# Late conditioning products at steps 3 to 28, 59 and 64 of the second block's input product, weights rounded one piece a step, and GpSimd's loads in that order

## What is computed

```python
mod = c_act @ w_ada[l] + b_ada[l]          # 1024 x 6144 weights
sh1, sc1, g1, sh2, sc2, g2 = jnp.split(mod, 6, axis=-1)
h = rmsnorm(x, norm1_g[l]) * (1.0 + sc1[:, None, :]) + sh1[:, None, :]
proj = h @ w_in[l]                         # 1024 x 5120 weights
q_m, k_m, v_m, q_d, k_d, v_d, gate_m, gate_d = jnp.split(proj, IN_SPLITS, axis=-1)
# rotary embedding on q_m, k_m, q_d, k_d; causal attention of both kinds;
# merged = sigmoid(gate_m) * y_m + sigmoid(gate_d) * y_d; x = x + g1 * (merged @ w_out)
# then a mixture of 32 experts, each with three matrices of 2 MB, and a last norm
```

## Time and profile before

| | |
|---|---|
| median of 3 runs | 1083.11 us (1081.07 to 1083.81) |
| profiled execution | 1078.99 us, span 1077.2 us |
| mean granted clock of TensorE | 0.946 |
| TensorE busy | 914.2 us (85%) |
| VectorE busy | 540.8 us (50%) |
| ScalarE busy | 347.3 us (32%) |
| DMA | 316.71 MB, mean 294 GB/s |

### The profile page before, as it was taken

How to read it: one execution, slowest core, us unless ns; L and a number is a source line. 1 busy time by engine, 2 the same in 40 slices (tenths; PEclk the granted TensorE clock), 3 DMA queues, 4 the chain that set the end, 5 groups by cost and what they waited for, 6 DMA issues and landing times.

```text
span 1077.2 us, 19224 instructions
## 1 busy us (share of the span) xinstructions
PE 914.2 (85%) x8378; PEld 703.1 (65%) x8378; DVE 540.8 (50%) x1008; ACT 347.3 (32%) x684; POOL 76.3 (7%) x113
## 2 busy tenths in 40 slices
PE   8999999999999999999999998766666666657665
PEld 7587888489999888988989965433334333334332
DVE  2465588858888766888757643211112111212121
ACT  3420255247776536455553341000001000000001
POOL 3111710000000000330010000000000000000000
PEclk9999999999999999999999999988889788988888
DMA  9434472685554564875536999999999999999994
GB/s 343 148 138 145 148 257 83 231 277 173 176 164 176 201 236 182 271 241 193 176 130 243 429 389 415 428 427 431 428 429 426 430 430 429 428 430 427 427 431 195
DMA packets 76106, 316.71 MB, mean 294 GB/s; under 512 B 3999, under 2 KB 27840, under 8 KB 63472
## 3 DMA queue, kind: packets, MB, share of 16 engines
q1 hardware_dynamic: 71252, 302.24, 71.4%
q0 software_dynamic: 4624, 13.14, 4.0%
q10 hardware_dynamic: 140, 0.04, 0.0%
HBM read 312.24 MB, written 1.06 MB: 291 GB/s over the span
## 4 chain that ended last, share of the span: by engine, by line
PE 56%; DMA 29%; DVE 8%; ACT 4%; issue 2%; SPq 1%; POOL 0%; DVEq 0%; ACTq 0%
PE ps L463 54%; DMA w<-in_w_up 20%; DMA w<-in_w_gate 6%; DMA w<-in_w_down 2%; DVE sp L1861 1%; DMA w<-in_w_in 1%; DMA rot<-q 1%; PE ps L589 0%; PE ps L2703 0%; DVE acc L925 0%; ACT sp L1852 0%; ACT sd L2184 0%; PE ps L2116 0%; SPq L3003 0%; SPq L3028 0%
## 5 line engine op out<-in xcount | busy, mean ns | idle before, releaser
L463 PE MATMUL ps<-w,xg 128*32 128x256 f32 x2048 | 158.1, 472 | 106.4 <-DMA w<-in_w_up 83.1
L463 PE MATMUL ps<-hb,sp 128*128 128x256 f32 x1824 | 224.6, 283 | 0.0
L463 PEld LDWEIGHTS ps<-hb,sp 128*128 128x128 f32 x1824 | 218.7, 188 | 3.9 <-issue 2.8
L463 PEld LDWEIGHTS ps<-w,xg 128*32 128x32 f32 x2048 | 84.4, 131 | 178.9 <-issue 154.7
L1861 DVE TENSOR_TENSOR sp<-w,sp 128x1024 fp32r<-128x1024 f32 x122 | 144.4, 1219 | 37.1 <-ACT sp L1852 37.1
L1852 ACT ACTIVATE sp<-w 128x1024 fp32r<-128x1024 f32 x122 | 122.1, 1051 | 41.5 <-PE ps L463 40.5
L2877 DVE TENSOR_TENSOR cst<-ps,cst 64x256 f32<-64x256 f32 x31 | 13.3, 428 | 222.2 <-ACT cst L2797 222.2
L2797 ACT ACTIVATE cst<-ps 64x256 f32<-64x256 f32 x31 | 11.7, 378 | 324.0 <-PE ps L463 324.0
L2903 DVE TENSOR_TENSOR ost<-ps,cst 32x256 f32<-32x256 f32 x120 | 50.4, 420 | 101.0 <-PE ps L463 98.2
L463 PE MATMUL ps<-w,hts 128*32 128x256 f32 x1024 | 63.0, 386 | 13.4 <-ACT hts L2810 11.4
L463 PE MATMUL ps<-ht,w 128*128 128x256 f32 x256 | 60.4, 386 | 2.8 <-ACT sq L709 1.7
(11 more groups left out here) (415 smaller groups left out, 1163.1 us busy)
## 6 DMA issues: line engine op xcount, KB each, us to landing
w<-in_w_down SPq DMA_DIRECT2D x36, 2048.0 KB, 35.2
w<-in_w_gate SPq DMA_DIRECT2D x32, 2048.0 KB, 28.2
w<-in_w_up SPq DMA_DIRECT2D x32, 2048.0 KB, 32.6
w<-in_w_in SPq DMA_DIRECT2D x13, 2048.0 KB, 9.9
w<-in_w_up SPq DMA_DIRECT2D x22, 1024.0 KB, 7.7
w<-in_w_ada SPq DMA_DIRECT2D x8, 2048.0 KB, 8.0
w<-in_w_out SPq DMA_DIRECT2D x4, 2048.0 KB, 9.1
w<-in_w_ada POOLq DMA_DIRECT2D x8, 768.0 KB, 5.0
```

Of the source, the lines that this page charges most:

```text
L463: return q.eng.matmul(o, l, r, start=start, stop=stop, skip_group_check=True)
```

## The change

Parts 4 to 11 of the late conditioning products are run by VectorE at steps 3, 8, 13, 18, 23, 28, 59 and 64 in place of 3, 11, 19, 27, 35, 43, 51 and 59. ScalarE rounds the second piece of a half one step after the first. GpSimd's order becomes: loads 0 to 6, rotation 2, load 7, rotation 3, load 8, rotation 4, load 9, rotation 5, load 10, rotations 6 to 9, load 11.

```diff
+        LATE_AT = (3, 8, 13, 18, 23, 28, 59, 64)
...
         def proj2_sc(q):
...
-                if g % 4 == 0 and 0 < g <= 80:
-                    split_sc(q, 35 + g // 4)
+                if g % 4 < 2 and 0 < g // 4 <= 20:
+                    split_sc(q, 35 + g // 4, (g % 4,))
...
         def proj2_ve(q, late_ada):
...
-                if g % 8 == 3:
+                if g in LATE_AT:
                     next(late_ada, END)
                 if g % 4 in (1, 2) and 0 < g // 4 <= 20:
                     split_ve(q, 35 + g // 4, (g % 4 - 1,))
...
         # GpSimd
-            for n in range(6):
+            for n in range(7):
                 ada_late_gp(q, n)
-            rotate_gp(q, 2)
-            for n in range(6, 9):
-                ada_late_gp(q, n)
-                rotate_gp(q, 2 * n - 9)
-                rotate_gp(q, 2 * n - 8)
-            ada_late_gp(q, 9)
-            rotate_gp(q, 9)
-            for n in (10, 11):
-                ada_late_gp(q, n)
+            for r in range(2, 6):
+                rotate_gp(q, r)
+                ada_late_gp(q, r + 5)
+            for r in range(6, 10):
+                rotate_gp(q, r)
+            ada_late_gp(q, 11)
             router_gp(q)
```

## The result

The changed kernel takes 1095.31 us (median of 5 runs, 1093.96 to 1096.87), the kernel before 1083.11 in the 5 runs beside them (1080.59 to 1085.32). The ratio is 1.0124, with a 95% interval of 1.0109 to 1.0139: slower; the medians are 12.2 us apart, and the interval is 11.8 to 15.1 us. The forecast was 1088.0, +4.9, in a range that ended at 1094.0. The direction was right; the size was less than half of what came, and the time lies 1.3 us above the range.

What follows compares the result with a forecast made beforehand. TensorE was taken as full to 465.52, with VectorE's rotary half 5 due then without slack. Delay 6.3, plus clock 0.7, less 1.05 and 1.0, gives +4.9 us: 1088.0 from 1083.11, range 1081.0 to 1094.0.

Steps and rivals of the forecast that it cites:

- the landing of loads 6 to 9: GpSimd's late loads, issue to landing: 6.0 us for 768 KB and 4.3 for 512 KB in the middle estimate.
- the loop: Load n waits for product n-1, VectorE for the load: 7.2 to 9.4 us a 768 KB link against 7.1 of room.
- my middle case: Late loads land in 6.0 us (512 KB: 4.3), load 6 at 444.1; rotary half 5 is 6.4 us late at step 31.
- My high case: Late loads land in 7.0 us (512 KB: 4.8), half 5 is 9.3 late; with 2.3 for rotation 6, +11.3 in all.
- These 2 MB loads start up to 8 us later and still land before their pieces are due: The step's own input-weight loads, delayed by late pieces, would be in time even at 12.7 us of landing.
- Rotation 6 behind load 10: Rotation 6, now issued behind load 10, might land late too: 2.3 us, counted only in the high sum.
- The 1.05 behind product 9: TensorE's other idle time between 465.52 and 503.90, behind product 9 on VectorE, should go: -1.05 us.
- the 1.0 from ScalarE's pd: TensorE's 1.28 us wait for ScalarE's pd at 544.60 should fall by one rounded piece: -1.0 us.
- The 1.34: TensorE's 1.34 us wait at 477.71 for VectorE's normalisation, expected to fall away against the clock's cost.
- The clock: After some 6 us of stall at step 31 TensorE's lower clock costs 2.0 us, net 0.7 less the wait at 477.71.
- The shift one for one: A TensorE delay at the end of the 84 steps reaches the kernel's end whole, as the experts' stream shifts with it.
- The 3.8 us for 768 KB: Skill's rule for late loads, 2.0 us plus bytes at 436 GB/s: half 5 only 1.2 us late, kernel 1080.6.

Runs made afterwards that it cites:

- e1_split_only: Kernel before with only ScalarE's second rounded piece one step later: 1080.8 us against 1082.88, ratio 0.9991.
- e3_rot_first: Changed kernel with each GpSimd rotation issued ahead of the load it stood behind: 1094.79 us against 1081.07 for the kernel before, ratio 1.0127.
- e7_late_end: Kernel before with the rounding edit, products 8 to 11 at steps 59, 64, 69, 74, loads 9 to 11 behind all rotations: 1080.53 us, ratio 0.9987.
- e6_two_places: Changed kernel with loads 5, 7 and 9 in a second place, so load n waits for product n - 2: 1083.07 us, ratio 1.0006 to the kernel before.
- e10_all_small: Changed kernel, loads 5 to 10 and input weights of halves 39 to 46 cut to 64 of 512 columns: scores +0.3 us, end of steps -2.4.
- e2_late_only: Changed kernel with ScalarE rounding both pieces in one step again: 1096.38 us against 1082.88 for the kernel before, ratio 1.0117.
- e4_small_loads: Changed kernel with loads 5 to 10 cut to 64 of 512 columns: 1088.03 us against 1082.88 for the kernel before, ratio 1.0045.
- e9_filler17: Changed kernel with 17 unused fp32 matmuls in TensorE's wait before the first scores: 1095.7 us against 1080.81 for the kernel before, ratio 1.0133.
- e11_cut4: Changed kernel with the 2 MB input-weight loads of halves 39 to 46 issued as four 512 KB loads: 1094.73 us, ratio 1.0111 to the kernel before.
- e12_cut8: Changed kernel with the 2 MB input-weight loads of halves 39 to 46 issued as eight 256 KB loads: 1096.37 us, ratio 1.0144 to the kernel before.

## Why the forecast was right in kind and wrong in size

**The step that failed** is the landing of loads 6 to 9, taken at 6.0 us (4.3 for load 8). They took 8.8, 6.1, 6.6 and 6.6. With these four put into the prediction's own links, from the issue of load 6 at 438.68 on, half 5 ends at 477.6; it ended at 477.7. So the loop and its other terms were right, and this one was mis-sized.

| | forecast (middle) | measured |
|---|---|---|
| waits at steps 8, 13, 18, 23, 28 | 2, 4, 1, 0, 1 | 2.06, 6.92, 1.11, 1.61, 2.75 |
| loads 6 to 9 issued | 438.1, 446.5, 455, 461.8 | 438.68, 449.85, 458.62, 467.11 |
| half 5 late at step 31 | 6.3 | 11.9 |

Load 6 brings 2.8 of the 5.6 us that were missing at step 31, loads 8 and 9 the most of the rest: load 8 had been taken as in time, and 1.61 us were waited for it. (The loss at the end of the steps, 12.9, is 8.0 above the forecast; the other 2.4 lie behind the scores, where 1.35 should have come back and 1.0 was lost. They are told below.) I had the row for load 6 in the earlier trace rows (7.0 us, beside a 2 MB load), took a middle between it and the quickest, and read it as a price per load. It is a landing behind another transfer: the load issued 1.8 us earlier lands 1.2 us earlier at the median and no earlier in the execution profiled here, so that its price grows by a part or all of what it is moved forward. From the kernel before, 447.0 could have been read as the time near which load 6 lands, 2.9 us later than the 444.1 of my middle case; the six traces with the new order have 446.2 to 447.0. And 7.0 us was the least of four: with rotation 2 ahead of it load 6 took 7.6, 8.2 and 7.5 in e1_split_only, e3_rot_first and e7_late_end. My high case (7.0 for each load of 768 KB, 4.8 for load 8) reached 9.3 and was too low as well.

**"These 2 MB loads start up to 8 us later and still land before their pieces are due"** was wrong. VectorE's late pieces delay the load that takes their slot, from 441.12 to 451.85; behind load 7 it takes 11.7 us and lands at 463.5, where ScalarE has waited for it. ScalarE's timeline:

```profile
445.68 2.01 ACT L1852 ACTIVATE sp<-w 128x1024 fp32r<-128x1024 f32 x2 [1.82 <-DMA w<-in_w_in]
...
463.54 2.01 ACT L1852 ACTIVATE sp<-w 128x1024 fp32r<-128x1024 f32 x2 [6.20 <-DMA w<-in_w_in]
```

TensorE didn't run out of pieces there, as it stood before its scores. But load 8 (458.62) and load 9 (467.11) again met one of these loads in flight: from 458 to 460 us SyncE's queue has 371 records and GpSimd's 1. The loop keeps itself going: a late product delays a piece, the piece a 2 MB load, and that one the next late load.

**The loop itself** (load n behind product n - 1, VectorE in order, the rotary work behind it) was right, and the direction of the result with it: e6_two_places, which cuts it, takes away 10.7 of the 11.9 us; e10_all_small, which makes its links short, 11.6.

**Rotation 6 behind load 10**, the 2.3 us that only the high case held, came: VectorE waits 2.62 us for it and TensorE 2.18 at 492.45. e3_rot_first, which turns the order round, takes both away.

**What is given back.** TensorE's idle time behind the first scores was 3.67 and is 3.04 (2.18, 0.17, 0.35, 0.34). The 1.05 behind product 9 went but for 0.17; the 1.0 from ScalarE's pd came, less what a second such wait took, and was shown alone in e1_split_only. The 1.34 was to go and is replaced by the 2.18.

**The clock.** It fell to 0.50 within the wait of 8.06 us (the window 474 to 476 shows 0.67, 476 to 478 shows 0.50). From there 4 and 36 matmuls took 0.80 and 5.85 us; before, the same 4 took 0.49 and the 36 behind them 4.53. That is 1.6 us where I took 2.0, and with 0.6 less idle time it makes the 1.0 by which the loss grows from the scores (11.9) to the end of the steps (12.9). Whether it cost time here is open: at 492.45 TensorE waits for VectorE anyway. In e3_rot_first, without that wait, such a fall cost 1.85.

**The shift one for one.** The first expert load is issued at 578.37 before and 591.71 after, 13.3 us later, and over the runs the stage and the kernel go together: +12.9 and +12.2, e2_late_only +13.8 and +13.5, e4_small_loads +5.1 and +5.2, e6_two_places -0.5 and +0.2. The experts' stream absorbs nothing, as forecast.

**The 3.8 us for 768 KB** of the Trainium skill (DMA: Bandwidth & Descriptors, Anatomy of one DMA), by which half 5 would have been 1.2 us late: the quickest load of that size here took 4.8 us before, and 5.5 with the 2 MB loads cut. For 96 KB the same rule gives an estimate of 2.2 us, and the traces, with 2.5 on a free wire, come near to it.

## What to carry to other kernels

A load's time to landing in a trace isn't its price: read which transfers were issued before it and are still moving, and forecast the moment of landing. Moving the issue forward by 1.8 us brought that moment nearer by 1.2 at the median, and by nothing in the execution profiled. When loads and uses share one buffer in series, compare the distance between uses with the slowest landing seen beside the big transfers, not with the median, and follow what a delay does to those transfers themselves. If there must be room, a second buffer (-10.7 us at the scores here) or uses left where there is slack is worth more than smaller pieces or another order of issue.

## What the runs showed of the hardware

- A load of GpSimd's issued 2.5 to 4.4 us behind a 2 MB load of SyncE's waited for most of it: 96 KB took 6.8 us and 2.5 alone, and cutting the 2 MB into 4 or 8 loads let the late load through no sooner. It isn't a rule for every pair: in e6_two_places the two queues moved side by side, and 512 KB issued 3.45 us behind 2 MB landed 5.4 us ahead of them.
- The granted clock fell without a stall of TensorE ahead of it that the trace shows. In the profiled execution of the changed kernel these 8 matmuls of the router stage take 6.49 us, and the window 636 to 642 shows a clock of 0.51 with TensorE busy all the time:

```profile
636.27 6.49 PE L463 MATMUL ps<-x,cst 128*128 128x512 f32 x8
```

```profile
636.00:642.00 6.00, 6.00 (x10) 2.77 (x10) 4.55 (x23) 5.00 (x12) 0.54 (x1) 0.51 1.00 424
```

Before they took 3.68 us, and 3.68 again in e2_late_only, e3_rot_first, e11_cut4 and e12_cut8, where the scores are as late; but 6.57 in e9_filler17, 5.10 in e4_small_loads, and 5.38 in e7_late_end, where the scores are in time. So the 2.8 us of this execution belong to no part of the change, and what lowered the clock there isn't known.
